# Giving every second expert's down matrix its own place, and reordering the last two experts, in a decoder step with a mixture of experts

## The reference, cut to what matters

```python
logits = x2d @ router_w + router_b                 # 264 x 32
top_val, top_idx = lax.top_k(logits, 4); top_w = softmax(top_val)
for each expert e, on its own tokens xb:
    hgu = xb @ moe_w_gu[e] + moe_b_gu[e]           # 1024 x 2048 matrix, 8.39 MB
    gate, up = min(hgu[:, :1024], 7), clip(hgu[:, 1024:], -7, 7)
    act = (up + 1) * gate * sigmoid(1.702 * gate)
    out = act @ moe_w_down[e] + moe_b_down[e]      # 1024 x 1024 matrix, 4.19 MB
y[token] += weight * out
x = layernorm(2 ** 0.25 * x + y)
```

## Time and profile before

| what | value |
|---|---|
| median of 3 runs | 1236.38 us (1234.74 to 1236.74) |
| the profiled execution's own time | 1235.94 us |
| its span | 1234.2 us, so 1.74 us lie around it |
| TensorE (PE) busy | 1174.4 us, 95% |
| VectorE (DVE) / ScalarE (ACT) busy | 382.1 us / 280.1 us |
| moved by DMA | 456.97 MB, mean 370 GB/s |
| mean granted clock of TensorE | 0.986 of full speed |

### The profile page before, as it was taken

The page is one execution under the profiler, slowest core; times in us unless marked ns, Lnnn a source line. Parts: engine busy times, 40 slices in busy tenths (PEclk is TensorE's granted clock), DMA queues, the critical chain, the costliest instruction groups (busy, mean ns, idle before and its releaser), DMA issues.

```text
span 1234.2 us, 16622 instructions
## 1 busy us (share of the span) xinstructions
PE 1174.4 (95%) x6700; PEld 647.8 (52%) x6700; DVE 382.1 (31%) x722; ACT 280.1 (23%) x505; POOL 23.3 (2%) x47
## 2 busy tenths in 40 slices
PE   8999999999999999999999998999999999998995
PEld 8999889995434343435344443434343434343432
DVE  5888588753221212123212111121212121212124
ACT  5686454433201010101010110101110101010101
POOL 1000011001000000000000000000000000000000
PEclk9999999899999999998999998999999999999998
DMA  9745578976989999999999999999999999999993
GB/s 290 232 124 184 160 233 261 340 288 263 425 369 426 426 425 426 427 425 426 420 427 427 425 426 423 427 425 427 425 426 427 427 426 426 426 425 425 426 425 148
DMA packets 82509, 456.97 MB, mean 370 GB/s; under 512 B 6608, under 2 KB 45632, under 8 KB 48960
## 3 DMA queue, kind: packets, MB, share of 16 engines
q1 hardware_dynamic: 79632, 447.07, 89.1%
q0 software_dynamic: 2832, 9.28, 2.4%
HBM read 450.38 MB, written 5.95 MB: 370 GB/s over the span
## 4 chain that ended last, share of the span: by engine, by line
PE 61%; DMA 32%; DVE 4%; issue 2%; ACT 1%; SPq 0%; DVEq 0%; ACTq 0%
DMA gu_w<-in_moe_w_gu 31%; PE pool L982 22%; PE pool L899 10%; PE pool L625 5%; PE pool L626 5%; PE pool L627 5%; PE ub L856 5%; PE pool L919 1%; PE ob L930 1%; PE pool L887 1%; ACT wh L1050 1%; PE ob L993 1%; PE ub L819 1%; PE ub L993 1%; DMA dn_w<-in_w_in 1%
## 5 line engine op out<-in xcount | busy, mean ns | idle before, releaser
L982 PE MATMUL pool<-gu_w,arena 128*64 128x512 f32 x1920 | 428.7, 600 | 24.8 <-DMA gu_w<-in_moe_w_gu 24.1
L982 PEld LDWEIGHTS pool<-gu_w,arena 128*64 128x64 f32 x1920 | 137.3, 138 | 305.1 <-issue 249.8
L899 PE MATMUL pool<-dn_w,arena 128*64 128x512 f32 x992 | 219.6, 595 | 0.8 <-ACT arena L1240 0.8
L1722 DVE TENSOR_SCALAR arena<-pool 128x512 f32<-128x512 f32 x31 | 21.4, 692 | 629.1 <-PE pool L982 624.2
L625 PE MATMUL pool<-xh,wh 128*128 128x264 f32 x568 | 164.7, 290 | 1.4 <-DVE arena L1319 0.6
L627 PE MATMUL pool<-xh,wl 128*128 128x264 f32 x568 | 161.7, 285 | 0.0
L899 PEld LDWEIGHTS pool<-dn_w,arena 128*64 128x64 f32 x992 | 68.6, 137 | 130.8 <-issue 130.5
L1235 ACT ACTIVATE arena<-arena 128x512 f32<-128x512 f32 x32 | 20.2, 630 | 479.4 <-DVE arena L1722 479.4
L625 PEld LDWEIGHTS pool<-xh,wh 128*128 128x128 f32 x568 | 108.0, 190 | 8.1 <-issue 4.4
L626 PE MATMUL pool<-xl_most,wh 128*128 128x264 f32 x385 | 110.1, 286 | 0.0
L627 PEld LDWEIGHTS pool<-xh,wl 128*128 128x128 f32 x568 | 107.5, 189 | 0.0
(11 more groups left out here) (334 smaller groups left out, 785.0 us busy)
## 6 DMA issues: line engine op xcount, KB each, us to landing
gu_w<-in_moe_w_gu SPq DMA_DIRECT2D x124, 2048.0 KB, 22.3
dn_w<-in_moe_w_down SPq DMA_DIRECT2D x124, 1024.0 KB, 19.1
dn_w<-in_w_in SPq DMA_DIRECT2D x24, 1024.0 KB, 6.1
dn_w<-in_w_branch SPq DMA_DIRECT2D x8, 1024.0 KB, 5.6
gu_w<-in_moe_w_gu SPq DMA_DIRECT2D x8, 1024.0 KB, 8.5
gu_w<-in_state_gla POOLq DMA_DIRECT2D x8, 512.0 KB, 6.5
out_gla_sample<-gu_w POOLq DMA_DIRECT2D x8, 512.0 KB, 4.7
dn_w<-in_w_o SPq DMA_DIRECT2D x4, 1024.0 KB, 6.6
```

The source lines that it names most:

```text
L899: last = mm(DOWN[s * CAP:(s + 1) * CAP, :], act_t[:, k % 4, k // 4 * CAP:(k // 4 + 1) * CAP], block[:, s * HF:(s + 1) * HF], start=(k == 0 ...
L982: last = mm(out, xg[:, k, j * CAP:(j + 1) * CAP], gu_w[:, k, cols], start=False, stop=(k == NB - 1))
L1722: ts(gbuf, gate, LIMIT, None, ALU.min).then_inc(gclip, 1)
```

## The change

Three things are changed.

1. The four arena pieces are kept for the second matrix of every odd expert (`dn_odd`), and `dn_w` is for the even ones. A quarter of a second matrix is now requested when expert n - 2 has used its place, not expert n - 1. The semaphores `dn_in` are split in even and odd.
2. At the start the order of requests becomes: first of 1, first of 2, second of 2, second of 3, first of 3. From expert 4 on it is first of n, second of n, as it was. At the end the order is: first of 30, first of 31, second of 30, second of 31, then the layer norm rows.
3. In the last pair TensorE makes both first products, then both second ones. Side jobs stand between the halves. Expert 31 has its activated rows in a place of its own (`act_last`) and its output in another PSUM bank (`DOWN_LAST`, the bank of `UP`); the sums of the single tokens move to the bank `ACTT`.

```diff
-        early = [blocks(slot(i, 0, 2 * D), 2) for i in (5, 3, 6, 0)]
+        dn_odd = [blocks(slot(i, 0, 2 * D), 2) for i in (5, 3, 6, 0)]
...
+        act_last = slot(1, 0, HF).rearrange("p (c s) -> p c s", c=4)
...
-        FIND, SUMD = GATE[:, 0:QD], UP[:, 0:2]
+        FIND, SUMD = GATE[:, 0:QD], ACTT[:, 0:2]
+        DOWN_LAST = UP
...
-            def load(n, e):
+            def next_gu(n, e):
 
                 for k in range(NB // 2):
                     sp.wait_ge(gu_used, n * NB + 2 * k + 2 - NB)
                     load_two(k, e)
+
+            def next_dn(n, e, odd):
+
                 for k in range(NB // 2):
-                    sp.wait_ge(dn_used, n * NB + 2 * k + 2 - NB)
-                    load_dn(k, e)
+                    sp.wait_ge(dn_used, n * NB + 2 * k + 2 - 2 * NB)
+                    (load_odd if odd else load_dn)(k, e)
 
             def body(it, pair):
-                load(it * 2 + 1, pair * 2 + 1)
-                load(it * 2 + 2, 0 if pair is PAIRS - 1 else pair * 2 + 2)
-
-            for e in (1, 2):
-                for k in range(NB // 2):
-                    sp.wait_ge(gu_used, (e - 1) * NB + 2 * k + 2)
-                    load_two(k, e)
-            for k in range(NB // 2):
-                sp.wait_ge(dn_used, 2 * k + 2)
-                load_dn(k, 2)
-
-            at = moe_loops(sp, body)
-            load(at * 2 + 1, E - 1)
-            sp.wait_ge(gu_used, (at * 2 + 1) * NB + 1)
+                for j in range(2):
+                    e = j if pair is PAIRS - 1 else pair * 2 + 2 + j
+                    next_gu(it * 2 + 2 + j, e)
+                    next_dn(it * 2 + 2 + j, e, j)
+
+            next_gu(1, 1)
+            next_gu(2, 2)
+            next_dn(2, 2, 0)
+            next_dn(3, 3, 1)
+            next_gu(3, 3)
+            n = moe_loops(sp, body, last=PAIRS - 2) * 2 + 2
+            for j in range(2):
+                next_gu(n + j, E - 2 + j)
+            for j in range(2):
+                next_dn(n + j, E - 2 + j, j)
+            sp.wait_ge(gu_used, (n + 1) * NB + 1)
...
+            def last_pair(it):
+                n = it * 2
+                pe.wait_ge(xg_ready, it)
+                expert_bias(n)
+                up_products(n, 0, range(NB))
+                add_former(it)
+                up_products(n + 1, 1, range(4))
+                pe.wait_ge(wpicked, it + 1)
+                pe.wait_ge(scat_read, it * 5 + 1)
+                turn_weights(scat_last)
+                for s in range(2):
+                    final_rows(FIN[0][s], s, 0, P)
+                up_products(n + 1, 1, range(4, NB))
+                final_rows(FIN[1][1], 1, P, P)
+                pe.wait_ge(swt_last, 1)
+                final_rows(FIN[1][0], 0, P, P)
+                down(n, it, 0, own=range(4))
+                pe.wait_ge(gclip, n + 2)
+                pe.wait_ge(gu_read, n + 3)
+                for c in range(NB):
+                    row, col = c // 2 * 32, c % 2 * P
+                    mm(FIND[row:row + DEC, col:col + P], yacc[:, c, SEQ:T], ident[:, :],
+                       start=(c % 2 == 0), stop=False, skip_group_check=True)
+                turn_act(n + 1)
+                down(n, it, 0, own=range(4, NB))
+                down(n + 1, it, 1, out=DOWN_LAST, act_rows=act_last)
...
+            sigmoid(n)
+            turned_act(n)
+            sigmoid(n + 1)
+            turned_act(n + 1, act_last)
+            sc.wait_ge(scat_done, it * 5)
+            output_rows(n, 0)
+            sc.wait_ge(dn_used, n * NB + 2 * NB)
+            nc.scalar.copy(eo[CAP:2 * CAP, 0:HF], DOWN_LAST[0:CAP, :]).then_inc(eo_last[0], 1)
```

More of the change, by code:

```diff
@@ L323, in build @@
         gu_in = [sem(f"gu_in{k}") for k in range(NB // 2)]
-        dn_in = [sem(f"dn_in{k}") for k in range(NB // 2)]
+        dn_in = [[sem(f"dn_in_{w}{k}") for k in range(NB // 2)] for w in ("even", "odd")]
         gu_used, dn_used = sem("gu_used"), sem("dn_used")
@@ L377, in settle, with moe_loops @@
                 self.eng.wait_ge(self.s, self.base + self.n)
-        def moe_loops(eng, body, amid=None):
+        def moe_loops(eng, body, amid=None, last=PAIRS - 1):
             with eng.Fori(1, MIDDLE if amid else PAIRS // 2) as pair:
@@ L396, in moe_loops @@
             rest = over * ((PASSES - 1) * PAIRS)
-            with eng.Fori(PAIRS // 2, PAIRS - 1) as pair:
+            with eng.Fori(PAIRS // 2, last) as pair:
                 body(rest + pair, pair)
-            return rest + (PAIRS - 1)
+            return rest + last
         block = ctx.enter_context(nc.Block())
@@ L418, in load_dn, with load_odd @@
                 sp.dma_start(dn_w[:, 2 * k:2 * k + 2, :], w_down[0, bass.ds(e, 1), 2 * k * P:(2 * k + 2) * P, :]
[L419 to L424, removed]
+                             .rearrange("e (p a) n -> (e p) a n", a=2)).then_inc(dn_in[0][k], 16)
+            def load_odd(k, e):
+                sp.dma_start(dn_odd[k], w_down[0, bass.ds(e, 1), 2 * k * P:(2 * k + 2) * P, :]
+                             .rearrange("e (p a) n -> (e p) a n", a=2)).then_inc(dn_in[1][k], 16)
             def load_x(half):
@@ L449, in _ @@
                     wait_drained(sp, f"b1{NB - 1}")
-                    load_early(0)
+                    load_odd(0, 1)
                 if i == len(tiles) - 5:
@@ L471, in _ @@
                     wait_drained(sp, f"b0{NB - 1}")
-                    load_early(1)
+                    load_odd(1, 1)
                     wait_filled(sp, f"b0{NB - 1}")
@@ L478, in _ @@
             wait_drained(sp, f"wo{NB - 1}")
-            load_early(2)
+            load_odd(2, 1)
             sp.wait_ge(lgt_full, 1)
-            load_early(3)
-            def load(n, e):
+            load_odd(3, 1)
+            def next_gu(n, e):
                 for k in range(NB // 2):
@@ L889, in turn_act, with down @@
                 last.then_inc(act_tr, 1)
-            def down(n, weights=dn_w, count=None):
+            def down(n, it, odd, out=DOWN, act_rows=act_t, own=range(NB)):
                 pe.wait_ge(actt_ready, n + 1)
[L894 to L897, removed]
+                if out is DOWN:
+                    pe.wait_ge(eo_ready, n + 1)
+                for k in own:
+                    pe.wait_ge(dn_in[odd][k // 2], it * 16 + 16)
+                    block = dn_odd[k // 2][:, k % 2, :] if odd else dn_w[:, k, :]
                     for s in range(2):
-                        last = mm(DOWN[s * CAP:(s + 1) * CAP, :], act_t[:, k % 4, k // 4 * CAP:(k // 4 + 1) * CAP],
+                        last = mm(out[s * CAP:(s + 1) * CAP, :], act_rows[:, k % 4, k // 4 * CAP:(k // 4 + 1) * CAP],
                                   block[:, s * HF:(s + 1) * HF], start=(k == 0), stop=(k == NB - 1))
@@ L931, in first_pair @@
                     last.then_inc(gu_used, 1)
-                down(0, dn_w, 32)
+                down(0, 0, 0)
                 turn_act(1)
@@ L941, in first_pair @@
                 turn_weights(scat_done)
-                down(1, early, 32)
+                down(1, 0, 1)
             def amid():
@@ L971, in amid @@
                 pe.wait_ge(mid_read, 2 * NB + 1)
[L973 to L1020, removed]
@@ new lines, in up_products, with add_former @@
+            def up_products(n, j, blocks_):
+                for k in blocks_:
+                    pe.wait_ge(gu_in[k // 2], n * 16 + 32)
+                    for out, cols in quarters(GATE, UP):
+                        last = mm(out, xg[:, k, j * CAP:(j + 1) * CAP], gu_w[:, k, cols],
+                                  start=False, stop=(k == NB - 1))
+                    last.then_inc(gu_used, 1)
+            def add_former(it):
+                pe.wait_ge(eo_ready, it * 2 + 1)
+                for d in range(4):
+                    if d == 2:
+                        expert_bias(it * 2 + 1)
+                        turn_act(it * 2)
+                    pe.wait_ge(scat_read, it * 5 - 3 + max(d - 1, 0))
+                    for x in range(2):
+                        last = mm((SCAT, SCAT2)[d % 2][:, x, 0:T], eo[:, (2 * d + x) * P:(2 * d + x + 1) * P],
+                                  swT, start=True, stop=True)
+                    last.then_inc(scat_done, 1)
@@ new lines, in body @@
+            def body(it, pair):
+                n = it * 2
[3 more added lines that the diff above has]
+                add_former(it)
+                down(n, it, 0)
+                up_products(n + 1, 1, range(NB))
+                pe.wait_ge(picked, it + 2)
+                pe.wait_ge(scat_read, it * 5 + 1)
+                gather(0, gath_done)
+                turn_act(n + 1)
+                gather(1, gath_done)
+                pe.wait_ge(wpicked, it + 1)
+                turn_weights(scat_done)
+                down(n + 1, it, 1)
@@ L1022, in _ @@
             first_pair()
-            body(moe_loops(pe, body, amid), PAIRS - 1, final=True)
+            at = moe_loops(pe, body, amid)
+            last_pair(at)
+            pe.wait_ge(eo_ready, at * 2 + 2)
```

(19 more changed lines are left out.)

2 lines of the change are left out of this document (1 added, 1 removed).

## The result

The changed kernel takes 1229.08 us (median of 4 runs, 1228.36 to 1230.36) against 1236.25 us before; the ratio is 0.9947 with a 95% interval of 0.9932 to 0.9962. The forecast was 1229.8, with 1228.4 to 1232.0 as its own range. The profiled execution, the slowest of the four, took 1230.36 us with a span of 1228.6, 5.6 us less than before.

The account below looks back on a forecast made before the run. DMA at 426 GB/s was taken to bound the kernel from 352 to 1210 us. Gains of 3.2 + 3.4 = 6.6 us took 1235.94 to 1229.3, with the median 0.44 higher: 1229.8; own range 1228.4 to 1232.0.

Parts of the forecast that it names:

- The bound: From 352 to 1210 us DMA moves 426 GB/s without a break; TensorE waits for weights, so its savings do not count.
- Part 1: Start of the stream: filling the DMA idle time gains 4.1 - 0.4 - 0.5 = 3.2 us, bounds 2.1 and 4.1.
- The idle stretch: From 346 to 352 us DMA moves 135 GB/s in place of 426; removing this gains 4.1 us.
- The tight place at 376 us: First request for expert 4: bytes flow at 376.5, queue dry at 376.7; 0.4 us lost, between 0 and 1.
- The place at 583 us: At `amid`, first request for expert 11 at 582.8, flow would end at 583.4; 0.5 us lost, between 0 and 1.
- Part 2: New order in the last pair: work after the last landing ends at 1212.8 in place of 1216.2, 3.4 us; bounds 2.4 to 3.6.
- The two paths end together: Last pair: TensorE's path and the path of the last landing both end at 1212.8 on the old time base.
- the rival that its path grows: Last pair: TensorE's path takes 3.4 us longer than summed, so only the start gains; 1233.2, chance 0.08.
- The 2.8 us said to return without cover: Last pair: VectorE's activation of 31 lies under 5.1 us of other work; without that, up to 2.8 us come back.
- Rival 1 and 2: 1: only the end gains, idle DMA returns at 376 or 583 us, 1233.0, chance 0.12. 2: only the start gains, 1233.2, 0.08.
- Rival 3: Whole stream: DMA rate falls 0.6% with the deeper queue or arena target, taking back 5 us; 1235.5, chance 0.06.
- Rival 4: Last pair: TensorE's clock falls amid small matmuls; 20 us at the lower level costs 10 us extra, 1239.8, chance 0.03.

Follow-up runs that it names:

- depth_as_before: Changed kernel, but second matrices of experts 4 to 29 wait for expert n - 1 again; 1228.73 us, ratio 0.9950 to the kernel before.
- front_only: Changed kernel with the new start, but the old order of requests and of TensorE's work at the end; 1231.96 us, ratio 0.9967 to before.
- the second profile: The changed kernel itself, measured and profiled again without any edit; 1228.78 us, ratio 0.9957 to the kernel before.
- down_first: Changed kernel, but from expert 4 on every second matrix is requested ahead of the first of the same expert; 1236.20 us, ratio 1.0010 to before.
- swap_four: Changed kernel, but for expert 4 alone the second matrix is requested ahead of the first; 1227.61 us, ratio 0.9947 to before.
- end_only: Changed kernel, but at the start the first matrix of 3 is requested ahead of the second of 3; 1231.82 us, ratio 0.9968 to before.
- pe_order_only: Changed kernel with TensorE's new order in the last pair, but the old order of requests at the end; 1237.49 us, ratio 1.0012 to before.
- request_order_only: Changed kernel with the new requests, but the old sequence on TensorE and ScalarE in the last pair; 1245.05 us, ratio 1.0077 to before.
- split_only: Changed kernel, but the last quarter of the second matrix of 31 is requested in two halves; 1229.28 us, ratio 0.9956 to before.

## Why the prediction was right, point by point

**The bound.** Right. From 352 to 1190 us the changed kernel moves 425 GB/s at a share of 1.01, and depth_as_before shows that a deeper queue in the middle of the stream is worth nothing.

**Part 1, 3.2 us.** Right in mechanism, and 3.3 by front_only's length. Its terms were off. The idle stretch gave (422 - 135) x 6 / 426 = 4.0 us, for 4.1. The tight place at 376 us took back 1.3 us, for 0.4 and a bound of 1. It took about as much in every profile with this order; the windows from 374 to 384 us of the second profile and of `front_only` both show 372 GB/s, (426 - 372) x 10 / 426 = 1.3 us. (The second profile's stage begins 1.4 us earlier, so a window from 376 us would miss the start of its dip.) The place at 583 us took nothing, for 0.5. These terms make 2.7 us in both profiles. That the sum of 3.2 came out so near is in part luck: one loss was too small by 0.9 us and the other too large by 0.5, and a length from one profile cannot tell 2.7 from 3.3. In the first profile TensorE waited twice for expert 9 after all, 0.31 and 1.26 us; in the second profile and in `front_only` it did not. Why is open, and it cost no request: the first one for 11 came at 583.04, for 582.8, and 3.1 us earlier than before in both profiles, counted from the first request of 3.

What was mis-sized is the new start of an almost empty queue. I counted idle time up to the first byte and took 0.4 us for a margin of 0.2. The first request for 4 came at 376.14, for 375.9, which left next to no margin against the dry point of 376.7. In the earlier trace rows the row from 350 has a share of 1.02 and only 197 GB/s, the next 0.54 and 131: after the start, two microseconds pass at about 40% of the rate, and (426 - 197 + 426 - 131) KB are 1.2 us, counted from 350.0. The row from 1169 of down_first has 1.18 and 229 GB/s in the same way. A margin near zero is paid with that ramp; this is my reading of the dip, since its 1.3 us are of the same size. Two other places had more room, by estimates worked out as the prediction did. At 583 us the request came 1.8 us ahead of the dry point (587.5 less the 2.7 us of the terms above). In `swap_four` the request of 404.3 came 1.9 us ahead of it (376.7 and the 29.5 us of an expert). Neither lost anything; no kernel set the margin by itself. The 0.6 us to a first byte of the Trainium skill ("DMA: Bandwidth & Descriptors", the specifications) may be so, but it is not all that a restart costs here: counted from 0.6 us after the request, at 350.2, the same rows still lack 1.0 us.

**Part 2, 3.4 us.** Right: 3.2 by end_only's length. In the change, the last quarter landed at 1208.6, 40.0 us after the last first-matrix quarter of 30, for 39.5 worked out (421 GB/s from 1190 on, for 426, is about 0.2 of it), and the products behind it took 1.96 us, for 1.77. "The two paths end together" was off by 0.9 us in TensorE's favour, so the rival that its path grows had 0.9 us more room than was said. The 2.8 us said to return without cover were a misreading. They are the time from the last product to the turn in the kernel before, and TensorE spent most of it on final rows and single tokens, work that is needed in either order. Its waits around the turn were 0.38 and 0.75 us.

**Rival 1 and 2**, only one part gains, fall with the change's 1229.08 us and with its windows and timeline. They put the end alone at 1233.0 and the start alone at 1233.2. Built as kernels, `end_only` gave 1231.82 and `front_only` 1231.96 where the kernel before had 1235.8, so 4.0 and 3.8 us less, for 3.4 and 3.2. **Rival 3**, a lower rate with the deeper queue, is refuted by 425 GB/s and by depth_as_before. I had said that if the queue took no more, SP would be held at a request that is not urgent. That is what happened (below), and it cost nothing. The Trainium skill (same page, on queues, rings and completion order) has the descriptors of one queue consumed in ring order; the trace agrees, since the last quarter, requested 32.5 us before its landing, came as the bytes ahead of it let it: by my estimate 11.7 MB were ahead, which with its own 1.05 MB take 30.3 us at 421 GB/s, and a quarter lands some 2 us after its bytes.

**Rival 4**, TensorE at its lower clock in the last pair, did not come in the change: the clock is 1.00 from 1172 to 1205, small matmuls and all. It did come in pe_order_only, behind the idle time of 5.66 us, and 32 products took 10.04 us for 7.04:

```profile
1183.00:1188.00 5.00, 4.71 (x12) 1.48 (x14) 0.00 (x0) 0.00 (x0) 0.00 (x0) 0.50 1.01 429
```

That is 1.2 GHz. In request_order_only the clock was 0.74 from 1188 to 1196, behind 13.30 us of waiting. So the drop exists, and it came behind a long wait, not behind the small matmuls that I had named. In pe_order_only it cost next to nothing: the last quarter of the first matrix of 31 was requested at 1172.14 and landed 25.8 us later, at 1197.9, and TensorE began it at about 1198.3 (half of the 7.0 us that start at 1194.80). At full clock it could have begun 0.4 us earlier at most. So that kernel's loss is the late data.

## What to carry to other kernels

When transfers bound a stage, look for the few microseconds in which they idle after it has begun, and for what stands behind the last landing; extra buffers in between earned nothing here. Put the requests in the order in which the consumer uses them, and change both orders together: here either one alone was worse than neither, by 0.1% and 0.8%, and both together were better. Before moving a request, work out for every place in the stream when the queue runs dry and when the next request can come, and leave it a microsecond or two: here about none lost 1.3 us, and an estimated 1.8 and 1.9 lost nothing. Then check both ends of the stream, since an order that fills a gap at one can open a larger one at the other.

## What was not expected of the hardware

SP can be held by a request when many are under way. Four requests of 1 MB took SP 2.1 us in the loop and 1.79 for expert 30, but the last four of the changed kernel took 5.58. Its requests from 1172 us:

```profile
1172.78 1.79 SPq L420 DMA_DIRECT2D dn_w<-in_moe_w_down  x4
1174.68 5.58 SPq L425 DMA_DIRECT2D arena<-in_moe_w_down  x4
1180.36 1.30 SPq L515 DMA_DIRECT2D gu_w<-in_ln_g  x1
1181.71 7.72 SPq L515 DMA_DIRECT2D gu_w<-in_ln_b  x1
```

One request of those four took 4.16 us by itself, and the one of `ln_b` took 7.72, where in the kernel before a quarter's request took 0.33 and that of `ln_b` 0.43. The second profile shows 4.17 and 8.95, so it is no accident of one execution. By my estimate from the landings, ten requests were not yet complete when the slow one was issued, and nine when the last of the loop's was, which was not held; the bytes under way were no more (about 11.7 MB for 12.5). So it seems to be a number of requests or descriptors, not bytes. `split_only` bears on it. There the first half of the last quarter stands at the same place in the list with half the bytes, and SP was held for the same 4.16 us. Its second half makes one request more, and the long hold came one request earlier, at `ln_g` (8.60 us) in place of `ln_b`. No run tells requests from descriptors.
